# A two-block attention, recurrence and expert kernel: three more places for streamed weights, and moves in the layers and the recurrence

## The reference

```python
def hybrid_layer(x, c, ...):                       # twice
    shift, scale, gate = split(c @ w_ada + b_ada, 3)
    h = split_cols((x * (1 + scale) + shift) @ w_in)
    # DSA: index scores relu(iq . ik) of 8 heads, weighted and summed, choose 64 keys a token
    isc = einsum("bth,bths->bts", iw, relu(einsum("bthd,bsd->bths", iq, ik)))
    o_dsa = attention over top_k(isc)              # 4 heads
    o_fox = causal attention with cumulated log-sigmoid decay    # 6 heads
    kc = silu(blocks(kc_in) @ w1) @ w2             # NSA: compressed keys and values
    o_nsa = g0 * compressed + g1 * selected + g2 * window        # 6 heads
    y = (concat(o_dsa, o_fox, o_nsa) * silu(h["gate"])) @ w_out
    return layer_norm(ALPHA * x + (1 + gate) * y)

def second_block(x, c, ctx, ...):                  # once
    mod, mod_c = silu(c) @ w_mod + b_mod, silu(c_ctx) @ w_mod + b_mod
    # context of 256 rows: only its two final states are wanted
    _, s_f, s_b = gdn_two_dirs(streams(norm(ctx) @ w_in), 0, 0)
    o, _, _ = gdn_two_dirs(streams(norm(x) @ w_in), s_f, s_b)
    x = x + gt1 * (concat(chunk_mlp(x), gdn_out(o)) @ w_out)
    # experts: each of 16 takes the 32 tokens with the largest softmax share
    aff = softmax(norm(x) @ w_router); gate, idx = top_k(aff.T, 32)
    for e in range(16):
        xe = x[idx[e]]
        ye[e] = (silu(xe @ w_gate[e]) * (xe @ w_up[e])) @ w_down[e] * gate[e]
    return rms_norm(x + gt2 * scatter_add(ye))
```

```python
v_new = u - w @ state
o     = q @ state + attn @ v_new
state = state * exp(g_last) + k_g.T @ v_new
```

## Time and profile before

| | |
|---|---|
| Three runs, median (lowest to highest) | 1399.01 us (1391.76 to 1400.58) |
| The profiled execution, its time | 1400.62 us |
| Its span, first to last instruction | 1398.8 us, 17315 instructions |
| TensorE busy (matmuls) | 1113.5 us, 80% of the span |
| VectorE, ScalarE, GpSimd busy | 432.1, 265.3, 70.0 us |
| Mean granted TensorE clock | 0.893 |
| Moved by DMA | 323.62 MB, 231 GB/s over the span |

### The profile page before, as it was taken

The page is one execution under the profiler, slowest core; times in us unless marked ns, Lnnn a source line. Parts: engine busy times, 40 slices in busy tenths (PEclk is TensorE's granted clock), DMA queues, the critical chain, the costliest instruction groups (busy, mean ns, idle before and its releaser), DMA issues.

```text
span 1398.8 us, 17315 instructions
## 1 busy us (share of the span) xinstructions
PE 1113.5 (80%) x7292; PEld 603.5 (43%) x7292; DVE 432.1 (31%) x1025; ACT 265.3 (19%) x604; POOL 70.0 (5%) x81
## 2 busy tenths in 40 slices
PE   2998799888979998999989989576666666666663
PEld 0444574444566447975679873421111111111111
DVE  0126546324644535353255471500000000000003
ACT  0102134121203425432121242100000000000002
POOL 1001000000000000002203300000000000000000
PEclk8999899989889999899988689697889988789887
DMA  9763138434226953113110002179999999999992
GB/s 378 298 240 121 61 128 334 155 122 143 98 74 257 429 206 133 52 74 117 62 61 3 2 1 107 43 300 427 428 427 427 427 428 428 428 426 428 427 428 123
DMA packets 24268, 323.62 MB, mean 231 GB/s; under 512 B 2704, under 2 KB 2704, under 8 KB 4864
## 3 DMA queue, kind: packets, MB, share of 16 engines
q1 hardware_dynamic: 22160, 314.18, 54.6%
q0 software_dynamic: 2032, 8.35, 1.7%
HBM read 321.47 MB, written 1.05 MB: 231 GB/s over the span
## 4 chain that ended last, share of the span: by engine, by line
PE 56%; DMA 29%; DVE 8%; issue 3%; ACT 3%; POOL 0%; SPq 0%; DVEq 0%; ACTq 0%; POOLq 0%
PE banks L584 47%; DMA ring<-in_stream 29%; PE banks L595 2%; PE banks L805 1%; PE banks L692 1%; PE banks L791 1%; PE banks L826 1%; PE banks L788 1%; PE banks L1958 1%; DMA grow<-in_rows 0%; DVE KC L1127 0%; PE banks L796 0%; DVE state L2216 0%; DVE small L1340 0%; DVE resid L1338 0%
## 5 line engine op out<-in xcount | busy, mean ns | idle before, releaser
L584 PE MATMUL banks<-ring,scr 128*32 128x512 f32 (+1 forms) x1088 | 176.4, 698 | 95.7 <-DMA ring<-in_stream 93.8
L584 PE MATMUL banks<-ring,uT 128*128 128x512 f32 (+1 forms) x512 | 230.0, 606 | 1.7 <-ACT uT L1415 1.1
L584 PEld LDWEIGHTS banks<-ring,uT 128*128 128x128 f32 x512 | 99.0, 197 | 119.5 <-issue 118.3
L584 PEld LDWEIGHTS banks<-ring,scr 128*32 128x32 f32 (+1 forms) x1088 | 42.7, 123 | 218.6 <-DMA ring<-in_stream 140.2
L584 PE MATMUL banks<-ring,zuv 128*32 128x512 f32 x512 | 88.2, 823 | 31.0 <-DMA ring<-in_stream 18.2
L2401 DVE SCALAR_TENSOR_TENSOR zuv<-zuv,banks 128x256 f32<-128x256 f32 x16 | 6.7, 422 | 306.7 <-ACT zuv L2654 306.7
L584 PE MATMUL banks<-scr 64*64 64x64 f32 (+2 forms) x2048 | 89.7, 241 | 6.6 <-DVE scr L2264 5.2
L584 PEld LDWEIGHTS banks<-scr 64*64 64x64 f32 (+1 forms) x2048 | 85.9, 150 | 12.9 <-issue 5.8
L584 PE MATMUL banks<-UWK,ring 128*128 128x256 f32 x320 | 74.6, 394 | 3.6 <-ACT UWK L2447 3.4
L595 PE MATMUL banks<-ring,KC 128*32 128x512 f32 x384 | 49.5, 641 | 28.4 <-DMA ring<-in_stream 28.4
L1958 PE MATMUL banks<-UWK,zuv 128*128 128x512 f32 x128 | 58.7, 602 | 16.5 <-DVE UWK L2407 16.5
(11 more groups left out here) (360 smaller groups left out, 1197.3 us busy)
## 6 DMA issues: line engine op xcount, KB each, us to landing
ring<-in_stream SPq DMA_DIRECT2D x148, 2048.0 KB, 15.9
w<-in_w POOLq DMA_DIRECT2D x2, 1024.0 KB, 9.6
probs<-in_rows POOLq DMA_DIRECT2D x4, 512.0 KB, 4.9
const<-in_consts SPq DMA_DIRECT2D x1, 1215.0 KB, 5.7
resid<-in_x SPq DMA_DIRECT2D x1, 1024.0 KB, 24.2
gate<-in_rows POOLq DMA_DIRECT2D x2, 512.0 KB, 12.1
zuv<-in_ctx POOLq DMA_DIRECT2D x1, 1024.0 KB, 7.4
grow<-in_rows POOLq DMA_DIRECT2D x2, 512.0 KB, 5.0
```

The source lines that it names most:

```text
L584: return pe.matmul(o, a, b, start=start, stop=stop)
```

## The change

**Three more places.** `slots()` gives each unit a place, the number of its use and the unit before it in that place. Units 0 to 51 keep their places. From the first expert's unit on, seven places go round: two of the ring, three new ones, two of the ring. The new ones lie in memory of the recurrence: `qk[:, 0:4096]` (free after the last query product, event `QS_mm` 3, 1), and two tiles that are laid out anew so that each is one piece of 4096: `Vt_to_O` (`Vt`, `attnT`, `state`, `O`) and `zuv_to_Kt` (`zuv`, `Kt`), both free after `mix2` 1, 1. What the experts kept there moves: `PgT`, `hT`, `hsil`, `hact`, `affT`, `selT` and `fin_row` to `UWK`, one selector to `qk`, and `Pg4` is left out, so the transposed selection of an expert is made by eight products of `Pg` with the identity, one for each quarter of the partitions and token tile. The load of `fin_row` waits for the router's product.

**Directions alternate.** In the state, query, key-value and attention products the loop over heads is outside, that over the two directions inside; waits for both directions stand ahead of each pair.

**Moves in the layers.** `v_cmp_hid` stands ahead of `v_h(5)` and `v_rope_k`; turn 6 uses bank 0; the index scores have four buffers; the output product finishes token tile 0 first and does all of the last quarter at the end. The diff also puts the transposes of token tile 1 (`pe_xT(pe, l, 1)`) behind the first product of tile 0.

```diff
--- before.py
+++ after.py
 RING = 4
+EXTRA = 3
...
+def slots():
+    order = unit_order()
+    first = next(k for k, u in enumerate(order) if u[0] == "pair")
+    late = [k % RING for k in range(first, first + RING)]
+    cycle = late[0:2] + list(range(RING, RING + EXTRA)) + late[2:]
+    slot = [k % RING if k < first else cycle[(k - first) % len(cycle)] for k in range(len(order))]
+    use, before, seen = [], [], {}
+    for k, b in enumerate(slot):
+        past = seen.setdefault(b, [])
+        use.append(len(past) + 1)
+        before.append(past[-1] if past else None)
+        past.append(k)
+    return slot, use, before
 def streamed(a):
...
-        relu = TB[:, B_FQ:B_FQ + 3, :].rearrange("p a s -> p (a s)").rearrange("p (a s) -> p a s", a=2)
+        relu = TB[:, B_FQ:B_FQ + 6, :].rearrange("p a s -> p (a s)").rearrange("p (a s) -> p a s", a=4)
...
-        zuv = sb("zuv", TILES, ZUV, stack=two)
-        zf = zuv[:, :, :].rearrange("p t d -> p (t d)")
-        Kt = sb("Kt", TILES, H2, HD2, stack=two)
-        Vt = sb("Vt", TILES, H2, HD2, stack=two)
+        zuv_to_Kt = sb("zuv_to_Kt", UNIT, stack=two)
+        zf = zuv_to_Kt[:, 0:TILES * ZUV]
+        zuv = zf.rearrange("p (t d) -> p t d", t=TILES)
+        Kt = zuv_to_Kt[:, TILES * ZUV:UNIT].rearrange("p (t h d) -> p t h d", t=TILES, h=H2)
+        Vt_to_O = sb("Vt_to_O", UNIT, stack=two)
+        Vt = Vt_to_O[:, 0:1024].rearrange("p (t h d) -> p t h d", t=TILES, h=H2)
...
-        attnT = sb("attnT", TILES, NDH, CH, stack=two)
-        state = sb("state", NDH, HD2, stack=two)
-        O = sb("O", TILES, B_W, stack=two)
+        attnT = Vt_to_O[:, 1024:2048].rearrange("p (t i n) -> p t i n", t=TILES, i=NDH)
+        state = Vt_to_O[:, 2048:3072].rearrange("p (i d) -> p i d", i=NDH)
+        O = Vt_to_O[:, 3072:4096].rearrange("p (t d) -> p t d", t=TILES)
...
-        selg = (selg, state[:, 0:2, :])
+        selg = (selg, qk[:, 4096:4352].rearrange("p (a n) -> p a n", a=2))
...
-        Pg4 = qk[:, 0:4096].rearrange("p (t e r s) -> p t e r s", t=TILES, e=EXPERTS, r=4)
...
+        fin_row = uwk[:, 3072:4096]
...
+        more = (qk[:, 0:UNIT], Vt_to_O[:, :], zuv_to_Kt[:, :])
...
-        fin_row = Kt[:, :, :, :].rearrange("p t h d -> p (t h d)")
...
-        def weights(k, n):
-            return ring[:, k % RING, 0:DCH * n].rearrange("p (k n) -> p k n", n=n)
+        slot, use, before = slots()
+        def held(b):
+            return ring[:, b, :] if b < RING else more[b - RING]
...
-            pe.wait_ge(K.sem(f"arrived{k % RING}"), 16 * (k // RING + 1))
-            return weights(k, n)
+            pe.wait_ge(K.sem(f"arrived{slot[k]}"), 16 * use[k])
+            return held(slot[k])[:, 0:DCH * n].rearrange("p (k n) -> p k n", n=n)
...
                     K.events["x_new", 0, 1] = K.events["x_new", 0, 0]
-                if k >= RING:
-                    sp.wait_ge(*at(*units[k - RING]))
-                sp.dma_start(ring[:, k % RING, :], A["stream"][k, :, :]).then_inc(*tick(f"arrived{k % RING}", by=16))
+                if before[k] is not None:
+                    sp.wait_ge(*at(*units[before[k]]))
+                elif slot[k] == RING:
+                    sp.wait_ge(*at("QS_mm", 3, 1))
+                elif slot[k] > RING:
+                    sp.wait_ge(*at("mix2", 1, 1))
+                sp.dma_start(held(slot[k]), A["stream"][k, :, :]).then_inc(*tick(f"arrived{slot[k]}", by=16))
             for t in range(TILES):
...
+        def turn_bank(n):
+            return 0 if n == 6 else n % 4
         def pe_turn(pe, l, n):
             dst, a, c, event, scale = list(turned(l))[n]
-            b = n % 4
+            b = turn_bank(n)
             pe.wait_ge(*free(b))
...
                     pe_y(pe, l, 1, 0, w_out, range(0, 5))
-            pe_y(pe, l, 1, 1, w_out, range(0, 5))
-            for t in range(TILES):
-                for cg in range(2):
-                    pe_y(pe, l, t, cg, w_out, range(5, DCH))
-                if l == DEPTH - 1 and t == 0:
-                    pe_ctx_T(pe)
+            for cg in range(2):
+                pe_y(pe, l, 0, cg, w_out, range(5, 7))
+            for cg in range(2):
+                pe_y(pe, l, 0, cg, w_out, range(7, DCH))
+            if l == DEPTH - 1:
+                pe_ctx_T(pe)
+            pe_y(pe, l, 1, 0, w_out, range(5, DCH))
+            pe_y(pe, l, 1, 1, w_out, range(0, DCH))
...
                 pe_ada_columns(pe, 0)
-            for t in range(TILES):
-                pe_xT(pe, l, t)
+            pe_xT(pe, l, 0)
             for cg in range(6):
...
                 pe_in(pe, l, cg, 0, w)
+                if cg == 0:
+                    pe_xT(pe, l, 1)
                 if cg == 3:
...
             for t, (lo, hi) in enumerate(((0, P), (P, 384))):
-                o, i, w = isc[:, lo:hi], relu[:, h % 2, lo:hi], small_iw[:, t, h:h + 1]
+                o, i, w = isc[:, lo:hi], relu[:, h % 4, lo:hi], small_iw[:, t, h:h + 1]
                 ins = (dve.tensor_scalar(o, i, w, None, ALU.mult) if h == 0 else
...
             v_turn(dve, l, 13)
+            v_cmp_hid(dve, l)
             v_h(dve, l, 5)
             v_rope_k(dve, l)
-            v_cmp_hid(dve, l)
             v_turn(dve, l, 3)
...
             act.wait_ge(*at("idx_mm", l, h))
-            if h >= 2:
-                act.wait_ge(*at("isc", l, h - 2, 1))
-            act.activation(relu[:, h % 2, :], bank[h % 4][:, 0:384], ACT.Relu).then_inc(*drain(h % 4, "relu", l, h))
+            if h >= 4:
+                act.wait_ge(*at("isc", l, h - 4, 1))
+            act.activation(relu[:, h % 4, :], bank[h % 4][:, 0:384], ACT.Relu).then_inc(*drain(h % 4, "relu", l, h))
             act.wait_ge(*drained(h % 4))
...
             pe.wait_ge(*free(0))
-            for r in range(2):
-                ins = pe_WS(pe, 0, r, n)
+            for h in range(H2):
+                for r in range(2):
+                    ins = pe_WS(pe, 0, r, n, h)
             ins.then_inc(*fill(0, "WS_mm", 0, n))
-        def pe_WS(pe, b, r, n):
+        def pe_WS(pe, b, r, n, h):
             t, p = at_step(n, r)
-            for h in range(H2):
-                i = r * H2 + h
-                c = slice(h * P, (h + 1) * P)
-                ins = mm(pe, bank[b][p:p + CH, c], WT[:, t, :, :].rearrange("p i (a c) -> p (i a) c", a=2)[
-                    :, wt_index(p, i), :], state[:, i, :], True, True)
-            return ins
-        def pe_KV(pe, b, r, n, v):
+            i = r * H2 + h
+            return mm(pe, bank[b][p:p + CH, h * P:(h + 1) * P], WT[:, t, :, :].rearrange("p i (a c) -> p (i a) c", a=2)[
+                :, wt_index(p, i), :], state[:, i, :], True, True)
+        def pe_KV(pe, b, r, n, h, v):
             t, p = at_step(n, r)
-            for h in range(H2):
-                ins = mm(pe, bank[b][:, h * P:(h + 1) * P], KG[p:p + CH, t, r * H2 + h, :], v(t, p, r, h), True, True)
-            return ins
+            return mm(pe, bank[b][:, h * P:(h + 1) * P], KG[p:p + CH, t, r * H2 + h, :], v(t, p, r, h), True, True)
...
+        def pe_both_KV(pe, s, n, where, v):
+            for b in where:
+                pe.wait_ge(*free(b))
+            for h in range(H2):
+                for r, b in enumerate(where):
+                    ins = pe_KV(pe, b, r, n, h, v)
+                    if h == H2 - 1:
+                        ins.then_inc(*fill(b, "KV_mm", s, n, r))
...
                 pe.wait_ge(*at("Vnew", 0, n))
-            for r, b in enumerate((4, 0)):
-                pe.wait_ge(*free(b))
-                pe_KV(pe, b, r, n, new_v if n else first_v).then_inc(*fill(b, "KV_mm", 0, n, r))
+            pe_both_KV(pe, 0, n, (4, 0), new_v if n else first_v)
...
                     pe.wait_ge(*at("state", *((1, n - 1, r) if n else (0, 3, r))))
-                    pe_WS(pe, r, r, n).then_inc(*fill(r, "WS_mm", 1, n, r))
+                for h in range(H2):
+                    for r in range(2):
+                        ins = pe_WS(pe, r, r, n, h)
+                        if h == H2 - 1:
+                            ins.then_inc(*fill(r, "WS_mm", 1, n, r))
                 for r in range(2):
-                    t, p = at_step(n, r)
                     pe.wait_ge(*free(2 + r))
-                    for h in range(H2):
+                for h in range(H2):
+                    for r in range(2):
+                        t, p = at_step(n, r)
                         ins = mm(pe, bank[2 + r][p:p + CH, h * P:(h + 1) * P], QT[:, h, t * P + p:t * P + p + CH],
                                  state[:, r * H2 + h, :], True, True)
-                    ins.then_inc(*fill(2 + r, "QS_mm", n, r))
+                        if h == H2 - 1:
+                            ins.then_inc(*fill(2 + r, "QS_mm", n, r))
                 for r in range(2):
                     pe.wait_ge(*at("Vnew", 1, n, r))
-                    if n < 3:
-                        pe.wait_ge(*free(4 + r))
-                        pe_KV(pe, 4 + r, r, n, new_v).then_inc(*fill(4 + r, "KV_mm", 1, n, r))
```

(27 more changed lines are left out.)

14 lines of the change are left out of this document (7 added, 7 removed).

## The result

The changed kernel took 1343.47 us (median of four runs, 1340.42 to 1344.98) against 1399.8 (four runs, 1391.76 to 1400.82): ratio 0.9607, 95% interval 0.9567 to 0.9647. It is 56 us faster; 1357.5 was forecast, with 1347 to 1370 as range. The profiled execution took 1344.98 us, span 1343.2, against 1400.62 and 1398.8.

What follows compares the result with a forecast made beforehand. The weight stream bounds the expert stage; TensorE and its waits bound everything earlier. The terms 14.8 + 8.0 + 16.8 - 5.6 + 4.6 + 3.0 = 41.6 us came off 1400.6; forecast 1357.5 on the median's scale, range 1347 to 1370.

Steps and rivals of the forecast that it cites:

- Three more places: Expert stage: three weight units on chip beforehand, 89 units left at an unchanged pitch of 4.93 us, 14.8 us earlier.
- Directions alternating: Both recurrences: passes of the two directions overlap, 3.0 us faster, 2.0 of it in the context's recurrence.
- The tokens' step: Tokens' recurrence: a step takes 6.6 us against 6.70, 0.1 for each of two steps, about 0.8 in the first.
- the deeper queue would slow the stream: Rival, chance 0.02, expert stage: open transfers hinder each other; at +0.6 us a unit the kernel takes 1411.
- Compression rows and bank: Each layer's attention: TensorE's waits of 4.63 and 2.40 us go, plus 1.4 of clock, 8.4 us a layer.
- index buffers: Each layer's index: four score buffers remove TensorE's 3.69 us wait ahead of the second half, 4.0 us a layer.
- Transposes: Each layer's first product: tile 1's transposes behind it leave TensorE waiting, a loss of 2.8 us a layer.
- Output order: Output product: tile 0's first half is complete earlier, 2.0 us won in layer 0 and 2.6 in layer 1.
- Layers together: Both layers: index buffers, compression rows, turn's bank, transposes and output order together, 23.8 us faster.
- The clock did give way: Rival, chance 0.12, denied this: only idle times go, transposes cost 3.9, output order gives nothing; 1369 us.
- the directions do overlap: Rival, chance 0.08, denied this in the recurrences: both directions wait for each other, -4 instead of +3; 1364.5 us.
- The order is not strict: Rival, chance 0.03, claimed the opposite: matmuls run in strict order, so alternating wins 4 x 0.95 more; 1353.7 us.

Runs made afterwards that it cites:

- `b_cmp_bank`: The kernel before with only the compression step moved ahead of the copy and turn 6 in bank 0: 1374.3 us, ratio 0.9855.
- upper group: The slower runs of the unchanged kernel before, 43 of 64, from 1395 us up, median 1400.6.
- `b_layers`: The kernel before with all layer edits, old order of the directions and four places: 1373.0 us, ratio 0.983.
- the last version: The changed kernel with layer 0's tiles both transposed first and, in layer 1, two tile 0 products ahead of tile 1's transposes: 1338.4 us, ratio 0.9549.

## Why the prediction was wrong

The direction, the stream's role and nearly every sign were right; the time missed by 14.0 us. On the traces the missed part lies at three places: 7.6 us in the directions (10.6 up to the experts where 3.0 were forecast), 3.4 in the expert stage (18.2 for 14.8) and 3.0 in the layers (26.8 for 23.8).

- **Directions alternating, 3.0 us: the term that failed.** Undone on the changed kernel it is worth 17.7 by the medians, and the traces of before and after show 12.5 by the end of the recurrence (4.4 in the context's levels, 6.5 in the 128 passes, 1.6 in the tokens' recurrence), 1.9 of them paid back before the experts. Two things are wrong in the step. First a size: of the context's key-value products I counted the first level's alone, and rounded down to 2.0; the rows gave 0.55 (1.71 to 1.16) and 0.46 (1.55 to 1.09) a level. Second, and larger, I did not look at the stretch at 1.2 GHz behind the context's recurrence, and so took it as fixed. Both traces of the kernel before have it, and against the trace of `b_cmp_bank` it costs 8.5 to 10.6 us; no trace with the context's products alternating has it, and with both alternating the kernel before has at most one of 22 runs in its upper group. My forecast subtracted from an execution that had it. How many of the 43 upper runs had it too is not shown. The tokens' step was right: 6.3 to 6.4 us for 6.6, first pair 1.96 for 1.95, second 2.18 for 2.2, states 2.41 for 2.5; its first step, in part at the low clock before, went from 8.98 to 7.97 us, 1.0 for 0.8.
- **Three more places, 14.8.** The mechanism held: 89 issues, the rest under the idle stretch, first issue tied to the same matmul. The pitch was not the same (4.896, not 4.92): 89 x 0.024 = 2.1 us more, 16.9 by the windows and by the run without the places. The other 1.3 us of the stage are not the places' doing: from the first issue to the end the stage took 480.7 us in both traces of before, but 479.3 and 479.5 in `b_layers` and `b_cmp_bank`, with four places too. That the deeper queue would slow the stream is refuted: the stage moves 426 GB/s. The Trainium skill, SBUF — State Buffer, summary for kernel authors, would have given 17.6 by its rate (an estimate), close to the total and for another reason: the units here land 4.90 us apart and not 5.9.
- **Compression rows and bank, 8.4 a layer, and index buffers, 4.0.** Waits gone as said, DVE not caught up. Together 15.5 us a layer on the traces where 12.4 were forecast. In layer 0 the surplus comes from a second product that had been at the low clock; in the second trace of before it was not, and others were. Only the first gate product's clock had been looked up, and that in one execution.
- **Transposes, -2.8 a layer.** 5.5 and 4.1 locally: the hole was sized right (1.04 and 1.86), the low clock fell on the product ahead of it and not behind it. At the end it is 3.1 by the times, and 5.8 or 9.5 by the traces, against the first or the second one of the changed kernel. The sum's 5.6 lies among these by luck, as its local sizes were too small.
- **Output order, 2.0 and 2.6.** 2.4 and 3.1 on the traces. Undone it is 4.6 by the end of layer 1, 7.4 at the end of the trace and 10.4 by the medians; what goes beyond 4.6 lies in code that is the same.
- **Layers together:** 23.8 forecast, 26.8 on the traces, 23.4 on the times. Undone one by one on the changed kernel, the others come to 17.7 + 18.7 + 13.9 + 10.4 - 3.1 = 57.6 us without the compression and bank edits, which alone bring 22; the whole is 56. The single prices are not independent and must not be added; that they overlap through the clock is likely, and only seen for the long stretch.
- **Rivals.** The clock did give way, and the directions do overlap. The order is not strict either: with a strict order the first pair of a step would have become 1.5 us shorter, and it became 0.54 shorter (2.50 to 1.96). In the trace before, the first query product starts ahead of state products that stand before it in the program:

```profile
818.62 0.32 PE L584 MATMUL banks<-state,QKT 128*64 128x128 f32 x1
818.72 0.27 PE L584 MATMUL banks<-state,UWK 128*64 128x128 f32 x1
```

  So "nothing is reordered", as the part on the engines says, does not hold for the starts of TensorE's products on different column halves. That they start strictly in order was the rule of the Trainium skill, TensorE: Matmul & The Clock Gate, Part 3, and the trace goes against it here.

## What to carry to other kernels

Before subtracting from a profile, look at how the times of the unchanged kernel are grouped and which group the profiled execution is of: a stretch at low clock in a dense part of it may be an event of that run and not of the program. Price a change of gaps with the clock rows of every product around it, ahead of the gap and behind. Do not read a difference of 3 or 4 us between two traces as the work of an edit before two traces of one kernel have been compared: those of the changed kernel end 3.7 us apart. And as single prices do not add up where the clock is part of the gain, measure edits together.

## What was not expected of the hardware

The 128 passes of 64 x 128 took 10.50 us at 2.4 GHz, about 12.3 with short low stretches, and 18.8 to 19.0 at 1.2 GHz, with the same code and the same inputs, behind 24 us at 2.4 GHz that were 99% busy in both the first and the last case. Of six traces with the old order in both of the context's products five have the long stretch; of the twelve with an alternating one none has. Why the order matters although the code behind it is the same is not settled. In the five the low clock sets in 0.8 to 1.0 us behind the first of the 128 passes. With both products alternating it sets in 4.8 to 5.1 us behind it in nine traces, for 3.4 us at first, and 10.2 us behind it in the last version's. No run shifts the 128 passes in time and leaves the order alone, so whether the order itself counts, or only the moment at which the passes come, is untested. And the tiles of the new places are filled 0.05 us a unit faster than the ring (4.84 and 4.89), which no run explains.
